# Gated memory: its denominators by a ones matrix that stays in the array while the weights move through it, four heads in rows, turned into columns at the end

## What is computed

```python
def mlstm_chunkwise(q, k, v, i_pre, f_pre):
    ...
        S = jnp.einsum('bhtd,bhsd->bhts', qb, kb) * jnp.exp(D - m_t[..., None])
        scale = jnp.exp(inter - m_t)
        num = jnp.einsum('bhts,bhsv->bhtv', S, vb) + scale[..., None] * jnp.einsum('bhvk,bhtk->bhtv', C, qb)
        den = jnp.sum(S, axis=-1) + scale * jnp.einsum('bhk,bhtk->bht', n, qb)
        h = num / jnp.maximum(jnp.abs(den), jnp.exp(-m_t))[..., None]
```

## Time and profile before

| | us |
|---|---|
| median of three runs | 3628.22 |
| profiled execution, span | 3611.2 |
| median less span | 17.0 |
| TensorE busy | 3494.6 (97%) |
| VectorE busy | 1444.0 (40%) |
| ScalarE busy | 1008.6 (28%) |
| GpSimd busy | 1499.2 (42%) |
| memory stage, first layer, from the first numerators to the first product with `w_out` | 2432.92 to 2470.00 |
| the same, second layer | 3162.59 to 3200.01 |

### The profile page before, as it was taken

The page is one execution under the profiler, slowest core; times in us unless marked ns, Lnnn a source line. Parts: engine busy times, 40 slices in busy tenths (PEclk is TensorE's granted clock), DMA queues, the critical chain, the costliest instruction groups (busy, mean ns, idle before and its releaser), DMA issues.

```text
span 3611.2 us, 41939 instructions
## 1 busy us (share of the span) xinstructions
PE 3494.6 (97%) x16800; PEld 2803.5 (78%) x16800; DVE 1444.0 (40%) x2493; ACT 1008.6 (28%) x1254; POOL 1499.2 (42%) x505
## 2 busy tenths in 40 slices
PE   7999999899999999999999999989999999899999
PEld 6878777578887888765788886967888868678887
DVE  6464268744243423135301026854201168543010
ACT  2222322622223212213322233343212234432121
POOL 3445552035454545510254554501546545015453
PEclk9999999999999999999999999988999999889999
DMA  6444222024352433211123221201222222002222
GB/s 259 175 153 180 98 82 71 1 105 175 125 196 98 186 134 148 96 40 68 66 86 108 84 98 70 82 13 39 91 104 93 93 71 82 24 35 94 93 93 82
DMA packets 54876, 360.68 MB, mean 100 GB/s; under 512 B 6080, under 2 KB 6464, under 8 KB 17728
## 3 DMA queue, kind: packets, MB, share of 16 engines
q1 hardware_dynamic: 54720, 358.53, 27.4%
HBM read 356.41 MB, written 2.10 MB: 99 GB/s over the span
## 4 chain that ended last, share of the span: by engine, by line
PE 92%; DVE 4%; ACT 2%; issue 1%; POOL 1%; DMA 1%; SPq 0%; DVEq 0%; ACTq 0%; POOLq 0%
PE LP L518 82%; PE XB L518 9%; ACT E L1263 1%; PE LP L876 1%; DMA big<-w_ada 1%; POOL w_lo L1754 0%; DVE gain L2090 0%; PE XB L760 0%; DVE XB L1955 0%; PE XB L722 0%; ACT sq L1263 0%; DVE S L2254 0%; ACT big_r L1263 0%; DVE big L2132 0%; DVE big L2130 0%
## 5 line engine op out<-in xcount | busy, mean ns | idle before, releaser
L1754 POOL TENSOR_TENSOR w_lo<-ring,w_hi 128x2048 fp32r<-128x2048 f32 (+1 forms) x263 | 1125.5, 4280 | 720.7 <-ACT w_hi L1263 720.2
L518 PE MATMUL LP<-u_hi,w_hi 128*128 128x512 f32 x2480 | 987.3, 398 | 17.5 <-ACT u_hi L1263 14.5
L518 PE MATMUL LP<-u_hi,w_lo 128*128 128x512 f32 x2480 | 975.7, 393 | 0.0
L518 PE MATMUL LP<-u_lo,w_hi 128*128 128x512 f32 x2480 | 944.6, 391 | 0.0
L518 PE MATMUL LP<-big_r,w_hi 128*128 128x512 f32 x2432 | 750.5, 390 | 3.7 <-POOL w_lo L1754 2.9
L1263 ACT ACTIVATE w_hi<-ring 128x2048 fp32r<-128x2048 f32 (+1 forms) x263 | 468.8, 1782 | 839.1 <-PE LP L518 748.2
L518 PE MATMUL LP<-big_r,w_lo 128*128 128x512 f32 x1472 | 575.5, 391 | 0.0
L518 PEld LDWEIGHTS LP<-u_hi,w_hi 128*128 128x128 f32 x2480 | 471.8, 190 | 131.3 <-issue 35.2
L518 PEld LDWEIGHTS LP<-u_hi,w_lo 128*128 128x128 f32 x2480 | 471.3, 190 | 100.4
L518 PEld LDWEIGHTS LP<-u_lo,w_hi 128*128 128x128 f32 x2480 | 467.6, 189 | 94.8 <-issue 0.5
L518 PEld LDWEIGHTS LP<-big_r,w_hi 128*128 128x128 f32 x2432 | 456.0, 188 | 98.8 <-issue 2.7
(11 more groups left out here) (310 smaller groups left out, 3600.8 us busy)
## 6 DMA issues: line engine op xcount, KB each, us to landing
ada_in<-w_ada SPq DMA_DIRECT2D x66, 1024.0 KB, 4.8
ring<-w_in SPq DMA_DIRECT2D x22, 1024.0 KB, 4.8
ring<-w_gu00a SPq DMA_DIRECT2D x11, 1024.0 KB, 7.0
ring<-w_gu00b SPq DMA_DIRECT2D x11, 1024.0 KB, 6.6
ring<-w_gu01a SPq DMA_DIRECT2D x11, 1024.0 KB, 6.7
ring<-w_gu01b SPq DMA_DIRECT2D x11, 1024.0 KB, 6.7
ring<-w_gu10a SPq DMA_DIRECT2D x11, 1024.0 KB, 6.6
ring<-w_gu10b SPq DMA_DIRECT2D x11, 1024.0 KB, 6.9
```

The lines of the kernel that those rows point to most:

```text
L518: return pe.matmul(o, lhsT=lhsT, rhs=rhs, start=start, stop=stop)
L1754: gp.tensor_tensor(w_lo[:, slab % RING, 0:width], ring[:, slab % RING, 0:width], w_high(q, width).bitcast(F32), ALU.subtract).then_inc(s(" ...
```

## The change

The denominators are computed with the operands' parts exchanged. The stationary operand is now a 128 x 32 block of ones, and the weights move, up to 512 columns at once. The result is a row, the same in 32 partitions, so each head gets a quarter of `XB[2]`: 32 partitions, 512 tokens. At the end ScalarE copies `XB[2]` into `E[:, 0, :]`, and TensorE transposes it in four blocks back into `XB[2]`, after which the sums of head i stand in column 32i of each block. The transposes stand in `out_products` of slab 0, behind three of its six chunks. VectorE waits for them, and not for `m_out`, before the four small instructions, and reads columns 0, 32, 64, ... of `XB[2]`.

```diff
@@ weighted(n), TensorE
                     for j in range(2):
-                        for q in range(b, NB):
-                            o = 4 * q + 2 * cp + j
-                            last = mm(XB[2][:, o:o + 1], sn[:, j, blk(q - b)], cc("ones", 0, 1),
-                                      start=n == 0 and j == 0 and q == 0, stop=n == 2 * NB - 1 and j == 1)
+                        rows = slice(32 * (2 * cp + j), 32 * (2 * cp + j) + 32)
+                        last = mm(XB[2][rows, b * P:T], cc("ones", 0, 32), sn[:, j, 0:T - b * P],
+                                  start=b == 0, stop=b == NB - 1)
                     last.then_inc(s("m_out"), 1)
@@ TensorE
-                out_products(0, range(2, DC))
+                out_products(0, range(2, 5))
+                pl.got("den_copied")
+                for b in range(NB):
+                    last = pe.transpose(XB[2][:, blk(b)], E[:, 0, blk(b)], cc("ident"))
+                last.then_inc(s("den_cols"), 1)
+                out_products(0, range(5, DC))
                 pl.got("num_squared")
@@ ScalarE
                 act.wait_ge(s("m_out"), (l + 1) * 2 * NB)
+                f(E[:, 0, :], XB[2][:, :], ACT.Copy).then_inc(s("den_copied"), 1)
                 f(Z[:, 0:2, :], XBS[:, 0:2, :], ACT.Square).then_inc(s("num_squared"), 1)
@@ VectorE
-                dve.wait_ge(s("m_out"), u0 + 2 * NB)
-                den = XB[2][:, 0:16]
+                dve.wait_ge(s("den_cols"), l + 1)
+                den = XB[2][:, 0:T:32]
```

## The result

The changed kernel takes 3594.7 us (median of four, 3591.0 to 3598.7) against 3627.3 us for the kernel before in the same comparison; the ratio is 0.9915, with a 95% interval from 0.9894 to 0.9937. It is faster, by more than was forecast: 3604 us, with a range that ended at 3599. A second comparison gave 3593.2 against 3630.6 us, a ratio of 0.9896 (0.9873 to 0.9919). So 33 to 37 us were gained, where 23.9 were expected.

A forecast was written before the change was run, and what follows sets the result against it. TensorE at half clock was taken to bound the memory stage; 7.7 + 4.9 - 0.66 = 11.9 us a layer, 23.9 for two, took the span from 3611.2 to 3587.3; plus 17.0 gave 3604 us, range 3599 to 3617.

The forecast's parts named there:

- What bounds the stage: Memory stage: TensorE bounds it, 20.4 us at granted clock 0.50; behind about 2464 us VectorE sets the time.
- The denominators: Memory stage, steps 0 to 5: single-column rows of 13.1 us become 5.4 us, heads side by side; 7.7 us saved a layer.
- The clock: Memory stage: clock rises as before and does not fall again, so other products run faster; 4.9 us saved a layer.
- The end of the stage: Behind the stage: four transposes add 0.66 us a layer on TensorE; ScalarE's copy is covered by 1.2 us.
- Stage total: Memory stage: denominators and clock together save 12.6 us a layer, before the transposes' loss.
- the last one of the sum: Whole kernel: adds 17.0 us, median of runs above the profiled span, to 3587.3 us, giving 3604.3 us.
- The range: Whole kernel: 3599 to 3617 us, meant to hold 8 in 10; 5 us below for the forecast's own uncertainty.
- Heads in turn: Rival, memory stage: the two heads' products run one after the other; 3611.5 us, chance 17%.
- Low clock: Rival, memory stage: clock stays low about as long as before, 3622 us; only delayed, 3608 to 3622; chance 18%.
- Slower: Rival, memory stage: heads one after the other and clock low together; 3642 us, chance 6%.
- Next bound sooner: Rival, memory stage: VectorE's weights or ScalarE's exponentials delay TensorE, or the copy's cover fails; 3608 to 3611 us, chance 9%.

The follow-up runs named there:

- e_same_strip: Changed kernel with both heads' ones products on the same 32 array columns, four denominators left out; 3602.9 us, ratio 0.9924 to the kernel before.
- e_cols01: Changed kernel with steps 0 and 1 back to products of one moving column, first key block's part left out; 3609.6 us, ratio 0.9943 to the kernel before.
- e_wide32: Kernel before with 32 moving columns of ones in place of 1, no copy or transposes; 3614.1 us, ratio 0.9961 to the kernel before.
- e_quad: Changed kernel with the ones products of two steps issued together, four column strips following each other; 3592.9 us, ratio 0.9919 to the kernel before.
- e_none: Changed kernel without the ones products, denominators left out, copy and transposes kept; 3583.3 us, ratio 0.9885 to the kernel before.
- b_look2: Kernel before, unchanged, profiled a third time; span 3630.1 us, both memory stages 43.1 us.

## Why the prediction was right or wrong, point by point

- **What bounds the stage: right.** TensorE was busy all through at 0.50, and the gain came from there. At its end the gap of 0.85 us behind VectorE stayed. One reading is off: of VectorE's waits of 1.35 and 0.97 us only the second lies between 2460.92 and 2463.90, so 0.97 us and not 2.3 covered TensorE there. The sum does not use it.
- **The denominators: right.** 5.4 us a layer were reckoned for steps 0 to 5; the rows give 1.18 + 1.05 + 0.84 + 0.84 + 0.63 + 0.62 = 5.2, for 13.1 removed. The heads run side by side, and without that 4.4 us a layer are lost (e_same_strip). The traces agree with the Trainium skill ("TensorE: Matmul & The Clock Gate", Part 3), by which small products on different column strips run at once: four records take 1.05 us on two strips against 1.90 on one, and on four strips eight records take 0.99 us.
- **The clock: right in kind.** It rose 1.8 to 4.0 us into the four stages and did not fall again. e_cols01 shows that the rows of single columns bring it down and that the products beside them pay. That the single column is the whole cause is not shown: with 32 moving columns the clock still fell in one of two stages (e_wide32).
- **The end of the stage: right.** The copy was covered. The transposes took 0.60 us, or 0.36 from their start to the next row's, for 0.66 reckoned. The 275 ns that the Trainium skill gives for a transpose in a kernel (the same page, Part 4) agree with the duration of each of these records, 0.27 us; but they overlap and follow each other at 0.09 us, so four times 275 ns, as the prediction's estimate has it, is too much.
- **Stage total: right for the execution profiled.** 12.6 us a layer were reckoned for the stage itself, the transposes standing behind it; 12.9 and 13.4 came.
- **The step that failed is the last one of the sum**: "The median of the runs is 17.0 us above the profiled span, and I keep that." For the changed kernel the median lies 5.5 us above its profiled span (3594.7 and 3589.2). That is 11.5 us less; the span itself came 1.9 us above the 3587.3 of the sum, and the two give the miss of 9.6.
- **What the 17.0 us were made of.** 1.8 us lie around the span. The mean span of the five profiles of before is 3622.6 us, 11.4 above the first: 5.9 us of it in the two memory stages (80.3 against 74.5), which go with the change, and 5.6 in the rest (3542.3 against 3536.7), which stay. Both are time at half clock. By stretches of 2 us, the stages have 45 us of it in the three quick profiles, 72 and 85 in the others; the rest has about 153 us in the first profile, 160 to 174 in the four others, 160 and 168 in the changed kernel. The last 4 us or so, from the mean of the profiles to the median of the timed executions, no profile shows. So the other part of the same mistake is the price of the stage: 37.3 us, of one execution, in place of a mean of 40.2. With that mean, and the 24.3 measured after, the gain is 31.8 us and the forecast would have been 3596; the two-layer saving of 23.9 us was too small by about 8. The sign that stood there to be read was that the runs spread over 6 us and lay 15 above the profiled one, in a kernel whose clock rises and falls within its stages.
- **The range was too narrow at its lower end** for the same reason: it gave 5 us to the base, and the stage alone varies by 9 us a layer.
- **The rivals.** Heads in turn: refuted by the rows, and when forced it came at 3602.9, not 3611.5, since its sum starts from the same short stage and keeps the same 17.0 us. Low clock: it did not come in the four profiled stages of the changed kernel; its milder form, a late rise, came in e_quad and e_none. Slower: no. Next bound sooner: no; with no denominators at all the stage still shrank.

## What to carry to other kernels

In this kernel rows of matmuls with one moving column cost more than their own time: behind them TensorE went to its lower clock (10.1 us of it in e_cols01's second stage), and the products around them paid. Let the wide operand move, keep the ones in the array, and give each row of results its own columns of the array so that they run side by side (1.05 against 1.90 us here). Before a forecast is built on a single profile of a kernel whose clock changes within a stage, compare its device time with the others: if they lie apart, the stages to be changed may be of another length in them, and a profile or two more will tell.

## What was unexpected of the hardware

- The same stage of the same program takes 37, 43 or 46 us, by when the granted clock rises and falls in it; it is at 0.50 at the start of each. Both stages of an execution were of the same kind in all five profiles of before, but not in e_wide32 (32.1 and 37.6). Why they go together was not examined.
- Four fp32 products with 32 columns of weights each, on four column strips, run in 0.99 us for 512 columns each, no longer than two (0.98), both from start to start.
- 32 moving columns in place of 1 cost next to nothing where the weight loads fill the row (in the kernel before 1.86 us of loads in the first row of 1.95): twelve records at full clock take 1.52 us in e_wide32, 1.50 with one column in b_look2.
